# Two fused blocks on one core: who adds the partial sums of the first projection

## The chip, the cores and the metric

The kernel runs as one program on one core of one Trainium2 chip. The metric is the device time of one execution in microseconds (us), taken as the median of several runs. A separately profiled execution gives the trace.

## The reference, cut to what matters

The reference is a network block of two mixer layers (a spatial gating unit, then multi-head latent attention), followed by a second block with its own mixers and a feed-forward part. All of it is float32, for one sequence of 256 positions and a model width of 2048. The change lies in the first projection of the first layer only:

```python
h = rms_norm(x, pre_g[i]) * (1 + scale[:, None, :]) + shift[:, None, :]
u, v, z = jnp.split(h @ w_in, 3, axis=-1)          # w_in: 2048 x 12288
u = jax.nn.gelu(u, approximate=False)
v = layer_norm(jax.nn.gelu(v, approximate=False), norm_g)
```

`shift` and `scale` come from `silu(c) @ ada_w + ada_b`, so `h` is known only as far as the columns of `ada_w` have been summed up.

## The kernel before, in words

**Tiles.** The 256 positions are two tiles `t` of 128 partitions. A float32 product is made of three products: each operand is split into a rounded part `hi` and the rest `lo`, and TensorE adds `hi*hi`, `hi*lo` and `lo*hi` in one bank. The left side of the first projection is held as `a_hi` and `a_lo`. The weights come in slabs of 1 MB (512 rows by 512 columns) into the four places of `raw`; SP issues the loads (`load`, L389), and each waits until the slab four loads before it has been read. A slab of weights is two chunks of 1024 elements per partition. For each chunk `q` ScalarE rounds `hi` (`hi_next`, L565), VectorE subtracts to get `lo` (`lo_next`, L1222), and TensorE runs twelve matmuls (`pe_chunk`, L2237 and L2242), after which `chunk_used` rises. `hi` and `lo` hold four chunks each, so `hi` of chunk `q` waits until chunk `q-4` has been used.

**Phases.** The first 12 column blocks of 512 (eight for `v`, four for the first half of `u`) are computed in four phases, since a quarter of `h` is ready at a time: phase `p` runs all 12 blocks with the rows `4p` to `4p+3` of the 16 row tiles. So there are 48 groups `m = 12p + j`, counted from 0; group `m` is chunks `2m` and `2m+1`. Group `m` writes one of two pairs of banks in turn, and `pe_block` (L2247) waits on `acc_free` until the group before the last one has been read out of its banks. The text calls p = 0 phase 1, and so on to phase 4.

**Read-out.** In phase 1, ScalarE copies the two banks of a group to their place in `v` or `y` (`act_result`, L584). In phases 2 to 4, ScalarE copies the two banks to `stage`, and POOL adds `stage` to the place (`pool_take`, L2088). ScalarE copies group `m` right behind `hi` of chunk `2m+4`, as soon as the group's chunks are used.

**The order of the work** is written out by hand, one queue per engine. In iteration `m` ScalarE does `hi(2m+3)`, `hi(2m+4)`, the read-out of group `m`, and in phase 4 `gelu(j-1)` (L820). VectorE does `lo(2m+3)`, `phase_sum(m+1)`, `lo(2m+4)`, and then small work: in phase 2 copies of turned weights (L1565, L1566), at the end of a phase the next quarter of `h` (L1518 to L1528), in phase 4 the statistics of `v` (L1536). `phase_sum` handles one slab of `ada_w` with four multiply-adds (L1245, L1249), two of them in banks, and every fourth slab with a closing addition (L1254); it is there for j up to 7 of each phase, in phase 4 up to 3. TensorE also has short matmuls between groups (L2316 after j = 3 and 7, transposes L2467 in phase 2). The root and the scaling of the layer norm (L671, L813) stand in ScalarE's queue of phase 4 and POOL multiplies by the gain from then on.

Of the kernel before, what the change touches and what calls it, by code (L numbers as in the profile page):

```python
# [15 lines left out]
ALU = mybir.AluOpType  # L16
# [8 lines left out]
T = 2  # L25
S = 256
D = 2048
KT = D // P
W2 = 4096
NB = 512  # L30
EPS = 1e-6
RAWS = 4
CHUNKS = 4
# [74 lines left out]
PHASES, PHASE_W, PHASE_A, LAST_A = 4, 12, 8, 4  # L108
U_FIRST, U_LAST = 64, 80
FIRST = PHASES * PHASE_W  # L110
MIXED, HEADS_W = 128, 137


PARTIAL = 2 * 3 * PHASE_W
STAGED = PARTIAL + 2 * 59
BEFORE_FFN = STAGED - 8 * 8
LAST_BANKS = 0

# [122 lines left out]
def build(nc, d, out):  # L241
    ctx = ExitStack()
    with ctx:
# [330 lines left out]
        def act_result(act, n, dst, func=ACT.Copy, aset=None, width=NB, normed=False):  # L574

            act.wait_ge(chunk_used, n.chunk.at(CHUNKS))
            if normed:
                act.wait_ge(n_rstd, n.nrm.base)
            for t in range(T):
                s = n.acc.base // 2 % 2 if aset is None else aset  # L580
                if dst is None:
                    act.wait_ge(stage_free, n.stg.at(t + 1))
                to = stage[:, t, :] if dst is None else dst(t)
                nc.scalar.activation(to, ps[:, 2 * s + t, 0:width], func, scale=rstd[:, t:t + 1] if normed else 1.0).then_inc(acc_free, 1)  # L584
            n.acc.base += 2
            if dst is None:
                n.stg.base += 2
# [190 lines left out]
        def _(act):  # L778
# [36 lines left out]
            def gelu(j):  # L815

                for t in range(T):
                    act.wait_ge(stage_free, 2 + PARTIAL - 2 * PHASE_W + 2 * j + t + 1)
                    place = v[:, t, j * NB:(j + 1) * NB] if j < 8 else y[:, t, (j - 8) * NB:(j - 7) * NB]
                    nc.scalar.activation(place, place, ACT.Gelu).then_inc(rounded, 1)  # L820

# [4 lines left out]
            for p in range(PHASES):  # L826
                for j in range(PHASE_W):
                    act_steps(act, n, 2)
                    if p == 0 and j == 2:
                        act.dma_start(ws[:, :, :], d["sgu_w_s"][0].rearrange("g t s -> t g s")).then_inc(ws_landed, 16)  # L830
                    if p < 3 and j == 9:
                        modulated(p + 1)
                        if p == 2:
                            act.dma_start(gain[:, :], d["sgu_norm_g"][0].partition_broadcast(P)).then_inc(gain_landed, 16)
                    if p == 1 and j < 4:
                        place, name = [(rows[:, 0:128], "hg_norm_2"), (rows[:, 128:192], "q_norm_2"), (rows[:, 192:256], "k_norm_2"),
                                       (rows[:, 256:272], "sinks_2")][j]
                        act.dma_start(place, d[name][0].partition_broadcast(P)).then_inc(rows_landed, 16)
                    if p:
                        act_result(act, n, None)  # L840
                    else:
                        act_result(act, n, lambda t: v[:, t, j * NB:(j + 1) * NB] if j < 8 else y[:, t, (j - 8) * NB:(j - 7) * NB])
                    if p == 3 and j:
                        gelu(j - 1)
                        if j == 9:
                            act_root(act, n)
                        if j == 11:
                            scaled(0)
# [365 lines left out]
        def lo_next(dve, n, ahead=AHEAD):  # L1214

            q = n.chunk.base + ahead
            if q >= FFN_CHUNK:
                return lo_planned(dve, q)
            r = raw_of(q)
            dve.wait_ge(hi_ready, n.chunk.at(ahead + 1))  # L1220
            width = chunk_width(q)
            nc.vector.tensor_tensor(lo[:, q % CHUNKS, 0:width], raw[:, r % RAWS, q % 2 * CW:q % 2 * CW + width],  # L1222
                                    hi[:, q % CHUNKS, 0:width].bitcast(F32), ALU.subtract).then_inc(lo_ready, 1)
            if q % 2:
                n.raw.base += 1
# [266 lines left out]
        def _(dve):  # L1492
# [45 lines left out]
            def phase_sum(m):  # L1538

                j = m % PHASE_W  # L1540
                if m < FIRST and j < (PHASE_A if m < FIRST - PHASE_W else LAST_A):
                    ada_sum(dve, n, j % 4, (acc, acc_s)[j // 4], early)

            lo_next(dve, n, 0)
            ada_keep(dve, n, 0, 16)
            modulated(0)
# [4 lines left out]
            for p in range(PHASES):  # L1551
                for j in range(PHASE_W):
                    lo_next(dve, n)
                    n.chunk.base += 1
                    phase_sum(p * PHASE_W + j + 1)
                    lo_next(dve, n)
                    n.chunk.base += 1
                    n.acc.base += 2
                    if j == 5 or p < 3 and j == 8:
                        ada_keep(dve, n, 0, (4 * p + 4 if p < 3 else 32) + (16 if j == 8 else 0))  # L1560
                    if p == 1 and j % 2 and j < 9:
                        q = j // 2
                        dve.wait_ge(sp_turned, q + 1)
                        bank = ps[:, 4, :].rearrange("p (g t) -> p g t", g=4)
                        nc.vector.tensor_copy(wt[:, 4 * q:4 * q + 4, 64:128], bank[:, :, 64:128])  # L1565
                        nc.vector.tensor_copy(wt[0:64, 4 * q:4 * q + 4, 0:64], bank[0:64, :, 0:64]).then_inc(sp_kept, 1)  # L1566
                    if p < 3 and j == 8:
                        modulated(p + 1)
                    if p < 3 and j == 9:
                        split(p + 1)  # L1570
                    if p == 3 and 2 <= j < 10:
                        stats(j - 2)
                    if p == 3 and j == 9:
                        dve.wait_ge(v_ready, 16)
                        for t in range(T):
                            ins = nc.vector.bn_aggr(agg[:, 2 * t:2 * t + 2], cnt[:, t, :, :].rearrange("p a b -> p (a b)"))
                        then(dve, n, ins)
                        nc.vector.tensor_scalar(var[:, :], agg[:, :].rearrange("p (t k) -> p t k", k=2)[:, :, 1], 1.0, EPS, ALU.mult, ALU.add).then_inc(n_var, 1)
                    if p == 3 and j == 10:
                        dve.wait_ge(n_sd, n.nrm.base + 1)  # L1580
                        nc.vector.reciprocal(rstd[:, :], sd[:, :]).then_inc(n_rstd, 1)
                        n.nrm.base += 1
                        dve.wait_ge(n_rstd, n.nrm.base)
                        nc.vector.scalar_tensor_tensor(out=nmr[:, :], in0=agg[:, :].rearrange("p (t k) -> p t k", k=2)[:, :, 0], scalar=-1.0,
                                                       in1=rstd[:, :], op0=ALU.mult, op1=ALU.mult).then_inc(centred, 1)
# [487 lines left out]
        def pool_take(pool, n, op):  # L2073

            for t in range(T):
                pool.wait_ge(acc_free, n.acc.at(5 + t))
                pool.wait_ge(stage_free, n.stg.at(2))
                op(t).then_inc(stage_free, 1)
                n.stg.base += 1
            n.acc.base += 2  # L2080
# [6 lines left out]
        def tt(out_, a, b, op):  # L2087
            return nc.gpsimd.tensor_tensor(out_, a, b, op)  # L2088

        @block.gpsimd  # L2090
        def _(pool):
# [15 lines left out]
            def gained(k):  # L2107

                g = SPATIAL[k]
                for t in range(T):  # L2110
                    pool.wait_ge(ln_scaled, 2 * k + t + 1)
                    piece = v[:, t, g * NB:(g + 1) * NB]
                    tt(piece, piece, gain[:, g * NB:(g + 1) * NB], ALU.mult).then_inc(ln_done, 1)

            n.acc.base = 2 * PHASE_W
            for p in range(1, PHASES):
                for j in range(PHASE_W):
                    place = lambda t: v[:, t, j * NB:(j + 1) * NB] if j < 8 else y[:, t, (j - 8) * NB:(j - 7) * NB]
                    pool_take(pool, n, lambda t: tt(place(t), place(t), stage[:, t, :], ALU.add))
                    if p == 3 and j == 10:  # L2120
                        pool.wait_ge(gain_landed, 16)
                        gained(0)
            gained(1)
            for b in range(4):
                c = slice(b * NB, (b + 1) * NB)
# [297 lines left out]
        def cols(buf, k0=0):  # L2423
            return lambda t, k: buf[:, t, k0 + k * P:k0 + (k + 1) * P]

        @block.tensor
        def _(pe):
# [58 lines left out]
                pe_block(pe, n, A, extra=extra)  # L2486
            pe.wait_ge(vm_act, 8)
            pe.wait_ge(vm_vec, 8)
            pe_blocks_turning(pe, n, A, cols(v), PARTIAL, ada=True, more=True)
            pe_pairs(pe, n, A, 2, ada=True)  # L2490
            pe_blocks_turning(pe, n, B, cols(v, D), PARTIAL + 16, ada=True, stays=True)
            pe.wait_ge(ada_kept, 1 + n.ada.base)
            pe_gate_rows(pe, 0)
            def columns():
# [389 lines left out]
```

## Time and profile before

| what | us |
|---|---|
| median of 3 runs | 2517.88 |
| lowest and highest run | 2517.03, 2519.02 |
| the profiled execution | 2517.61 |
| its span in the trace | 2515.6 |

The span is what the trace covers; 2.0 us of the profiled execution lie around it. Engines are TensorE (PE, with its weight loads PEld), VectorE (DVE), ScalarE (ACT), GpSimd (POOL) and SyncE (SP). A group of instructions is named by its line in the kernel, its engine and its operands. An instruction's duration can reach into the next one's on the same engine, so that starts of neighbours stand closer than their durations.

### The profile page before, as it was taken

The page shows a single profiled execution, that of the slowest core. Times are in us where ns is not written, and L with a number is a line of the kernel's source. Part 1 is how long each engine was busy: PE and PEld are TensorE (multiplying, and loading weights), DVE is VectorE, ACT ScalarE, POOL GpSimd, SP SyncE. Part 2 cuts the span into 40 slices and gives each one's busy share as a digit, 9 for nine tenths or more (in the row PEclk, how much of TensorE's full clock was granted, in tenths as well). Part 3 has the DMA queues.
Part 4 walks back from the last instruction along what each step waited for, and adds up shares of the span by engine and source line. Part 5 has one row for each costly group of instructions (what it writes and reads, how often), then busy time and mean ns, then how long its engine had stood idle before and what let it go on. Part 6 is the DMA issues. An engine that isn't in the chain of part 4 may idle for free.

```text
span 2515.6 us, 31563 instructions
## 1 busy us (share of the span) xinstructions
PE 2465.0 (98%) x11802; PEld 2054.3 (82%) x11802; DVE 1872.2 (74%) x2280; ACT 1403.5 (56%) x1956; POOL 442.1 (18%) x290
## 2 busy tenths in 40 slices
PE   5999999999999999998999999999999999999999
PEld 4888888888887888887888888888888888888887
DVE  7899787866777777766665555557888879888884
ACT  4555764444446655546566667655555645545553
POOL 0065572111021000010000000043111111111111
PEclk9999999999999999999999999999999999999999
DMA  9989777878875877754555554554455564646454
GB/s 349 331 302 337 253 251 270 309 277 283 283 254 181 232 228 215 232 176 142 167 173 162 167 167 150 179 172 170 181 202 200 171 231 167 219 169 222 167 205 157
DMA packets 353477, 547.35 MB, mean 218 GB/s; under 512 B 30684, under 2 KB 124480, under 8 KB 352960
## 3 DMA queue, kind: packets, MB, share of 16 engines
q1 hardware_dynamic: 351520, 539.53, 63.4%
q10 hardware_dynamic: 1824, 6.04, 0.7%
q8 instruction: 84, 1.38, 0.2%
q14 instruction: 49, 0.40, 0.0%
HBM read 543.43 MB, written 2.10 MB: 217 GB/s over the span
## 4 chain that ended last, share of the span: by engine, by line
PE 91%; DVE 5%; ACT 2%; issue 1%; DMA 1%; SPq 0%; DVEq 0%; ACTq 0%; POOL 0%; POOLq 0%
PE ps L2237 50%; PE ps L2242 25%; PE ps L2267 2%; PE ps L2264 2%; PE ps L2263 2%; PE ps L2223 1%; PE ps L2222 1%; PE ps L2224 1%; PE ps L2316 1%; DVE ps L1245 1%; DVE lo L1199 1%; ACT hi L565 1%; DVE lo L1222 1%; PE ps L2840 1%; PE ps L2478 1%
## 5 line engine op out<-in xcount | busy, mean ns | idle before, releaser
L1222 DVE TENSOR_TENSOR lo<-raw,hi 128x1024 fp32r<-128x1024 f32 x550 | 707.7, 1303 | 386.5 <-ACT hi L565 385.7
L565 ACT ACTIVATE hi<-raw 128x1024 fp32r<-128x1024 f32 x550 | 572.3, 1051 | 434.0 <-PE ps L2242 353.2
L2237 PE MATMUL ps<-hi,a_hi 128*128 128x512 f32 (+1 forms) x2016 | 801.0, 397 | 1.2 <-DVE a_lo L1427 0.9
L2237 PE MATMUL ps<-hi,a_lo 128*128 128x512 f32 (+1 forms) x2016 | 785.8, 390 | 0.0
L2242 PE MATMUL ps<-lo,a_hi 128*128 128x512 f32 (+1 forms) x2016 | 539.0, 389 | 0.0
L551 ACT ACTIVATE hi<-raw 128x1024 fp32r<-128x1024 f32 x339 | 358.0, 1060 | 293.1 <-PE ps L2242 254.7
L1199 DVE TENSOR_TENSOR lo<-raw,hi 128x1024 fp32r<-128x1024 f32 x339 | 424.9, 1273 | 107.0 <-ACT hi L551 105.0
L2242 PEld LDWEIGHTS ps<-lo,a_hi 128*128 128x128 f32 x2016 | 378.4, 188 | 79.4
L2237 PEld LDWEIGHTS ps<-hi,a_hi 128*128 128x128 f32 x2016 | 379.0, 188 | 78.8 <-issue 1.9
L2237 PEld LDWEIGHTS ps<-hi,a_lo 128*128 128x128 f32 x2016 | 379.2, 188 | 74.3
L2237 PE MATMUL ps<-hi,b_hi 128*128 128x512 f32 x880 | 348.0, 395 | 0.6 <-ACT y L938 0.3
L2237 PE MATMUL ps<-hi,b_lo 128*128 128x512 f32 x880 | 343.3, 390 | 0.0
L2242 PE MATMUL ps<-lo,b_hi 128*128 128x512 f32 x880 | 235.8, 390 | 0.0
L2088 POOL TENSOR_TENSOR v<-v,stage 128x512 f32<-128x512 f32 (+1 forms) x88 | 149.1, 1695 | 421.8 <-ACT stage L584 281.5
L2242 PEld LDWEIGHTS ps<-lo,b_hi 128*128 128x128 f32 x880 | 165.2, 188 | 35.3
L2237 PEld LDWEIGHTS ps<-hi,b_hi 128*128 128x128 f32 x880 | 165.4, 188 | 34.3 <-issue 0.7
L2237 PEld LDWEIGHTS ps<-hi,b_lo 128*128 128x128 f32 x880 | 165.4, 188 | 33.1
L2088 POOL TENSOR_TENSOR v<-v 128x512 f32<-128x512 f32 x48 | 77.3, 1624 | 593.2 <-ACT v L744 304.7
L1245 DVE SCALAR_TENSOR_TENSOR ps<-raw,cond,ps 128x512 f32<-128x512 f32 x194 | 137.3, 746 | 1.5 <-DMA raw<-in_ada_w 1.5
L2088 POOL TENSOR_TENSOR x<-x,stage 128x512 f32 (+1 forms) x38 | 71.6, 1884 | 332.0 <-DVE stage L1442 310.6
L584 ACT ACTIVATE stage<-ps 128x512 f32<-128x512 f32 x120 | 65.0, 593 | 60.7 <-PE ps L2242 59.7
L2088 POOL TENSOR_TENSOR y<-y,stage 128x512 f32<-128x512 f32 x30 | 52.5, 1751 | 169.2 <-ACT stage L584 167.0
(343 smaller groups left out, 2532.7 us busy)
## 6 DMA issues: line engine op xcount, KB each, us to landing
raw<-in_ada_w SPq DMA_DIRECT2D x96, 1024.0 KB
raw<-in_sgu_w_in SPq DMA_DIRECT2D x96, 1024.0 KB
raw<-in_w_up SPq DMA_DIRECT2D x64, 1024.0 KB
raw<-in_w_down SPq DMA_DIRECT2D x64, 1024.0 KB
raw<-in_w_in SPq DMA_DIRECT2D x42, 1024.0 KB
raw<-in_sgu_w_out SPq DMA_DIRECT2D x32, 1024.0 KB
raw<-in_w_in SPq DMA_DIRECT2D x128, 256.0 KB
raw<-in_mla_w_in SPq DMA_DIRECT2D x32, 512.0 KB
```

Source lines behind the costliest of these rows:

```text
L551: nc.scalar.activation(by_rows(hi[:, q % CHUNKS, :]), raw_piece(place), ACT.Copy).then_inc(hi_ready, 1)
L565: nc.scalar.activation(hi[:, q % CHUNKS, 0:width], raw[:, r % RAWS, q % 2 * CW:q % 2 * CW + width], ACT.Copy).then_inc(hi_ready, 1)
L584: nc.scalar.activation(to, ps[:, 2 * s + t, 0:width], func, scale=rstd[:, t:t + 1] if normed else 1.0).then_inc(acc_free, 1)
L1199: nc.vector.tensor_tensor(by_rows(lo[:, q % CHUNKS, :]), raw_piece(place), by_rows(hi[:, q % CHUNKS, :]).bitcast(F32), ALU.subtract).then_ ...
L1222: nc.vector.tensor_tensor(lo[:, q % CHUNKS, 0:width], raw[:, r % RAWS, q % 2 * CW:q % 2 * CW + width], hi[:, q % CHUNKS, 0:width].bitcast( ...
L1245: ins = nc.vector.scalar_tensor_tensor(out=out[:, :] if a == j == 3 else to, in0=w, scalar=c, in1=to, op0=ALU.mult, op1=ALU.add)
L2088: return nc.gpsimd.tensor_tensor(out_, a, b, op)
L2237: nc.tensor.matmul(ps[:, 2 * s + t, 0:width], x[:, k0 + j, t * P:(t + 1) * P], hi[:, c, w], start=begins, stop=False)
L2242: ins = nc.tensor.matmul(ps[:, 2 * s + t, 0:width], x2[0][:, k0 + j, t * P:(t + 1) * P], lo[:, c, w], start=False, stop=last and j == kts - 1)
L2263: nc.tensor.matmul(ps[:, bank, :], left(j)[0], hi[:, c, w], start=begins and j == 0, stop=False)
L2264: nc.tensor.matmul(ps[:, bank, :], left(j)[1], hi[:, c, w], start=False, stop=False)
L2267: ins = nc.tensor.matmul(ps[:, bank, :], left(j)[0], lo[:, c, w], start=False, stop=ends and j == 1)
```

## The change

ScalarE's copies to `stage` and POOL's additions are gone in phases 2 to 4 of the first projection. VectorE reads each bank and adds it to the place in `v` or `y`. It does group `m-1` in iteration `m`, behind `lo(2m+4)`, and group 47 as well in the last iteration. The addition itself raises `acc_free`; `gelu` on ScalarE waits on `acc_free` in place of `stage_free`. POOL starts at the gain of the layer norm. The counts of `stage_free` are shifted by the additions that are gone (PARTIAL).

```diff
-PARTIAL = 2 * 3 * PHASE_W
-STAGED = PARTIAL + 2 * 59
+STAGED = 2 * 59
...
             def gelu(j):
                 for t in range(T):
-                    act.wait_ge(stage_free, 2 + PARTIAL - 2 * PHASE_W + 2 * j + t + 1)
+                    act.wait_ge(acc_free, 4 + 2 * (FIRST - PHASE_W + j) + t + 1)
...
                     if p:
-                        act_result(act, n, None)
+                        n.acc.base += 2
...
+            def partial_add(m):
+
+                j = m % PHASE_W
+                dve.wait_ge(chunk_used, CHUNKS + 2 * (m + 1))
+                if m == PHASE_W:
+                    dve.wait_ge(acc_free, 4 + 2 * PHASE_W)
+                for t in range(T):
+                    place = v[:, t, j * NB:(j + 1) * NB] if j < 8 else y[:, t, (j - 8) * NB:(j - 7) * NB]
+                    nc.vector.tensor_tensor(place, place, ps[:, m % 2 * 2 + t, :], ALU.add).then_inc(acc_free, 1)
...
                     lo_next(dve, n)
                     n.chunk.base += 1
                     n.acc.base += 2
+                    if p * PHASE_W + j > PHASE_W:
+                        partial_add(p * PHASE_W + j - 1)
+                    if p == PHASES - 1 and j == PHASE_W - 1:
+                        partial_add(p * PHASE_W + j)
...
-            n.acc.base = 2 * PHASE_W
-            for p in range(1, PHASES):
-                for j in range(PHASE_W):
-                    place = lambda t: v[:, t, j * NB:(j + 1) * NB] if j < 8 else y[:, t, (j - 8) * NB:(j - 7) * NB]
-                    pool_take(pool, n, lambda t: tt(place(t), place(t), stage[:, t, :], ALU.add))
-                    if p == 3 and j == 10:
-                        pool.wait_ge(gain_landed, 16)
-                        gained(0)
+            n.acc.base = 2 * FIRST
+            pool.wait_ge(gain_landed, 16)
+            gained(0)
             gained(1)
...
-            pe_blocks_turning(pe, n, A, cols(v), PARTIAL, ada=True, more=True)
+            pe_blocks_turning(pe, n, A, cols(v), 0, ada=True, more=True)
```

## Rows read from the trace of the kernel before

**Rows 1.** Page, part 1: busy us, share of span, instructions by engine.
```profile
PE 2465.0 (98%) x11802; PEld 2054.3 (82%) x11802; DVE 1872.2 (74%) x2280; ACT 1403.5 (56%) x1956; POOL 442.1 (18%) x290
```

**Rows 2.** Window: length; busy PE, PEld, DVE, ACT, POOL; PEclk, DMA share, GB/s.
```profile
117.57:315.05 197.48, 196.99 (x893) 163.18 (x893) 177.43 (x192) 125.15 (x176) 120.42 (x70) 1.00 0.85 298
```

**Rows 3.** Critical chain, TensorE's pieces: start us, length us, what.
```profile
92.65 1.81 PE ps L2237 x8
...
117.57 1.85 PE ps L2237 x8
...
120.34 1.81 PE ps L2237 x8
...
123.06 1.81 PE ps L2237 x8
...
225.33 0.84 PE ps L2316 x8
...
315.05 1.81 PE ps L2237 x8
```

**Rows 4.** Timeline, ScalarE: start us, us, what, idle before and its releaser.
```profile
92.74 1.06 ACT L565 ACTIVATE hi<-raw 128x1024 fp32r<-128x1024 f32 x1 [1.31 <-PE ps L2242]
...
122.52 1.06 ACT L565 ACTIVATE hi<-raw 128x1024 fp32r<-128x1024 f32 x1 [3.31 <-DMA raw<-in_sgu_w_in]
...
262.26 1.28 ACT L820 ACT_TABLE_LOAD   x1
263.56 1.16 ACT L820 ACTIVATE v<-v 128x512 f32<-128x512 f32 x2
```

**Rows 5.** Timeline, VectorE, the same columns.
```profile
93.84 1.23 DVE L1222 TENSOR_TENSOR lo<-raw,hi 128x1024 fp32r<-128x1024 f32 x1 [1.15 <-ACT hi L565]
94.98 0.15 DVE L1261 COPY mod<-ps 128x4 f32<-128x4 f32 x1
...
124.75 0.42 DVE L1565 COPY wt<-ps 128x256 f32<-128x256 f32 x1
...
125.53 1.54 DVE L1222 TENSOR_TENSOR lo<-raw,hi 128x1024 fp32r<-128x1024 f32 x1
...
129.74 0.69 DVE L1254 TENSOR_TENSOR acc<-ps,acc 128x512 f32<-128x512 f32 x1
130.35 1.21 DVE L1222 TENSOR_TENSOR lo<-raw,hi 128x1024 fp32r<-128x1024 f32 x1
...
191.54 2.72 DVE L1245 SCALAR_TENSOR_TENSOR ps<-raw,cond,ps 128x512 f32<-128x512 f32 x4
194.17 3.23 DVE L1222 TENSOR_TENSOR lo<-raw,hi 128x1024 fp32r<-128x1024 f32 x2
```

**Rows 6.** Timeline around one wait of TensorE for VectorE, the same columns.
```profile
809.97 0.42 DVE L1427 TENSOR_TENSOR a_lo<-tf,a_hi 128x256 fp32r<-128x256 f32 x1 [0.72 <-ACT a_hi L733]
...
810.45 0.50 PE L2237 MATMUL ps<-hi,a_hi 128*128 128x512 f32 x1 [0.65 <-DVE a_lo L1427]
...
810.78 0.39 PE L2237 MATMUL ps<-hi,a_lo 128*128 128x512 f32 x1
```

**Rows 7.** Groups of VectorE, 46 to 114 us (phase 1): count, busy us, mean.
```profile
L1222 DVE TENSOR_TENSOR lo<-raw,hi 128x1024 fp32r<-128x1024 f32 x26 | 31.2, 1221 | 9.4 <-ACT hi L565 9.4
L1245 DVE SCALAR_TENSOR_TENSOR ps<-raw,cond,ps 128x512 f32<-128x512 f32 x28 | 19.2, 749 | 1.5 <-DMA raw<-in_ada_w 1.5
```

**Rows 8.** Groups of VectorE and POOL in phase 3 (182 to 248 us).
```profile
L1222 DVE TENSOR_TENSOR lo<-raw,hi 128x1024 fp32r<-128x1024 f32 x24 | 40.3, 1716 | 2.0 <-ACT hi L565 1.8
L1245 DVE SCALAR_TENSOR_TENSOR ps<-raw,cond,ps 128x512 f32<-128x512 f32 x25 | 17.1, 743 | 0.0
...
L2088 POOL TENSOR_TENSOR v<-v,stage 128x512 f32<-128x512 f32 x16 | 23.1, 1446 | 20.3 <-ACT stage L584 19.1
```

**Rows 9.** Windows of 2 us where TensorE idled, columns as in rows 2.
```profile
794.00:796.00 2.00, 0.77 (x3) 0.30 (x2) 2.00 (x4) 1.37 (x6) 0.00 (x0) 1.00 0.25 21
...
1158.00:1160.00 2.00, 0.09 (x1) 0.12 (x1) 2.00 (x7) 1.93 (x8) 0.00 (x0) 0.50 0.00 0
```

More of the change, by code:

```diff
@@ L2488, in _ @@
             pe.wait_ge(vm_vec, 8)
-            pe_blocks_turning(pe, n, A, cols(v), PARTIAL, ada=True, more=True)
+            pe_blocks_turning(pe, n, A, cols(v), 0, ada=True, more=True)
             pe_pairs(pe, n, A, 2, ada=True)
-            pe_blocks_turning(pe, n, B, cols(v, D), PARTIAL + 16, ada=True, stays=True)
+            pe_blocks_turning(pe, n, B, cols(v, D), 16, ada=True, stays=True)
             pe.wait_ge(ada_kept, 1 + n.ada.base)
```

## The prediction, made before the changed kernel was run

> **What bounds the kernel now.** I read the page's first part, then a window over the stretch that the change touches, then the critical chain there, then the timelines of each engine for prices. The page shows TensorE busy for 98% of the span and POOL for 18% [rows 1]: time off ScalarE or POOL is worth nothing unless TensorE waited for it. The window runs from the start of group 13 to the end of phase 4, 197.48 us [rows 2]. TensorE is busy in 196.99 of them at a granted clock of 1.00, its upper level of 2.4 GHz. So there is half a microsecond to win and everything to lose. VectorE is already busy for 177.43 us of the same window. In the critical chain a chunk lasts from 120.34 to 123.06, that is 2.72 us, and a group 5.44 [rows 3]. The 35 groups 13 to 47 make 35 x 5.44 = 190.4 us; the other 7.1 are TensorE's own short work (five column sums of about 0.84 us and three sets of transposes) with its restarts.
>
> **What the change removes.** 72 copies leave ScalarE, which is no bound. 72 additions leave POOL. That helps VectorE: its `lo` subtraction, with both inputs in SBUF, takes 1716 ns in phase 3 while POOL adds, and 1221 ns in phase 1 where POOL is still; the multiply-add that works in a bank takes 743 and 749 [rows 7, 8]. In phase 3 this gives VectorE back 24 x 0.495 = 11.9 us. It is worth nothing by itself, since TensorE did not wait.
>
> **What it adds to VectorE.** Two additions of 128x512, one input in a bank. The nearest row is the closing addition, of the same form: 0.69 us, with the next instruction 0.61 behind its start [rows 5]. A pair is 1.30 us, 72 additions are 72 x 0.61 = 44 us of VectorE's queue, about 15 a phase. The lower bound is this row; above, half of a held-up `lo`, 0.86 us each [rows 8].
>
> **What it moves, the step that decides.** Group m+1 may start only when group m-1 has been read out. ScalarE used to do that while group m ran. Now VectorE does it in iteration m behind `lo(2m+4)`, which needs `hi(2m+4)`, which needs chunk 2m used. From the end of chunk 2m TensorE has only chunk 2m+1 to run, 2.72 us, and then needs the banks. In that time must pass, one after the other:
> - TensorE's end to ScalarE's start: chunk end 92.65, `hi` at 92.74, 0.09 [rows 3, 4];
> - `hi`, 1.06 [rows 4], and its end at 93.80 to `lo` at 93.84, 0.04 [rows 4, 5];
> - `lo` until VectorE takes the next instruction, 93.84 to 94.98, 1.14 [rows 5];
> - the two additions, 0.61 + 0.69 = 1.30 [rows 5];
> - VectorE's end to TensorE: 809.97 + 0.42 = 810.39 to 810.45, 0.06, and the first matmul takes 0.33 to the second instead of 2.72/12 = 0.23, together 0.16 [rows 6].
>
> This is 3.79 us against 2.72: TensorE stops for 1.07 us in every group, though nothing is overloaded. The next chunk follows, so the cycle of a group is 3.79 + 2.72 = 6.51. No lead helps: `hi(2m+4)` has no free place earlier. It holds for groups 14 to 48, which wait for the additions of groups 12 to 46: 35 cycles, 227.9 us.
>
> VectorE's own queue in a group with a slab of `ada_w`: from the end of chunk 2m+1 at 2.72, `hi(2m+5)` and signals, `lo(2m+5)` starts at 2.72 + 0.09 + 1.06 + 0.04 = 3.91, and the additions let go at 1.19 + 1.14 + 1.22 = 3.55, before it. Then 1.14 and four multiply-adds, 191.54 to 194.17, 2.63 [rows 5]: `lo(2m+6)` can start at 7.68, and the cycle wants it at 6.51 + 1.19 = 7.70. Both limits meet, so whatever is added to this queue now costs. Added are:
> - the closing addition (j = 2 and 6 in phases 2 and 3, j = 2 in phase 4): 5 x 0.61 = 3.1 us;
> - the copies in phase 2, 124.75 to 125.53, 0.78 [rows 5], start at 3.55 and push `lo(2m+5)` from 3.91 to 4.33: three times with a slab behind them, 3 x 0.42 = 1.3 us;
> - the first read-out: `hi(30)` came 122.52 - 120.34 = 2.18 us after chunk 26, held by its DMA, not 0.09 [rows 3, 4]: 2.1 us once. Later slabs have a longer cycle to land in, so I charge the DMA queue of SP nothing more; without that cover it is the DMA's pace of before, 5.44 a group, below the new cycle;
> - phase 4, j = 1 to 2: `gelu` now waits for VectorE's addition and ScalarE's `hi(2m+5)` stands behind it. The first addition ends at 1.19 + 1.14 + 0.69 = 3.02; a table load of 1.28 and two gelus of 1.16 [rows 4] end at 5.46, and `lo(2m+5)` starts at 6.56, not at 3.91. If the load is made ahead of the wait it is some 1.1 less. Behind it is the last slab sum: 1.5 to 2.6, I take 2.1. Without such a sum, in the other groups of phase 4, `hi(2m+5)` is done by 5.4 and `hi(2m+6)` only starts at 6.6, which hides gelus and statistics;
> - the root at j = 9 with its two tables: nothing to 2 x 1.28 = 2.6, I take 1.2, near one load [rows 4].
>
> These make 9.8 us. POOL's gain multiplications start earlier if at all, and the last two additions stand where VectorE used to wait for `hi(99)`: nothing, as long as the lead of three chunks is there; without it they cost their 1.3 us.
>
> **The sum.** The window becomes 227.9 + 9.8 = 237.7 us. TensorE's short work falls into the stops, so it is not added. Less 197.48 this is 40.2 us more. The profiled execution took 2517.61 (span 2515.6 and 2.0 around it); 2517.6 + 40.2 = 2557.8, and the median of the runs is only 0.3 above that execution. Nothing later gives it back, TensorE being full. I say 2558.
>
> **The rivals.** *Not slower.* The queues alone are counted: a group with a slab costs VectorE 2 x 1.14 + 2.63 + 1.30 = 6.21 against 5.44, eight groups a phase, 8 x 0.77 = 6.2 us behind, and a lead of three chunks, 8.2 us, swallows that before the light groups make it up. Then the banks come free in time and the run stays at 2518. It decides itself at 2.72 us from the end of chunk 2m to the second addition's end. For it: VectorE gets 11.9 us back. Against: the pieces of that path sum to 3.63 even without the restart, and the lead does not apply to it. 5%: 3 for no change, 2 for a small gain out of the time given back.
>
> *Half the stop.* Signals and restart cost nothing and part of `lo` is ready when the bank wait is looked at: 35 x 0.5 + 5 = 23 us, 2541. Against it stands each row above. 8%.
>
> *ScalarE gets stuck in phase 4.* If every gelu and every round of `hi` changes the table, 2 x 1.28 a group, less the 1.2 us that ScalarE has spare, cost 11 x 1.36 = 15 us more, 2573; with the additions at 0.86 each (35 x 0.5 = 17) it is 2590. The row shows a table load once there, not a load per group. 14%.
>
> *The clock falls.* TensorE now stops once a group. Where it idled longer the trace shows both: with 0.77 us busy in 2, the granted clock is 1.00; in 1158 to 1160, after several microseconds with little work, it is 0.50, the lower level of 1.2 GHz [rows 9]. Stops of 1.07 in 6.51 are far milder than the first, so I expect 2.4 GHz. If it fell every second cycle, two chunks of 5.44 would take the place of 6.51: 17 x 4.4 = 75 us more, 2633. 6%. The Trainium skill, page "TensorE: Matmul & The Clock Gate", section "A second HAM failure mode: psum-queue depth-cycling", says that short idles of TensorE between groups that take turns in the banks can make the clock go back and forth; by that rule this change would bring this case, and no row here shows it at such short stops.
>
> **Chances.** The forecast has 67%. Its own range: all signals and extras at their least give about 2542 (35 x 0.3 and 5 less), the additions at their upper bound 2575. Taking in half the stop and the first part of the stuck ScalarE, the range is 2538 to 2580. A measurement of this kernel tells some 0.2% (5 us) from no change. Faster 0.02, same 0.03, slower 0.95.
>
> **What would show it.** In the profile after: TensorE waiting for VectorE's additions into `v` and `y` some 35 times, about 1 us each; in the chain the pattern TensorE, `hi`, `lo`, two additions, TensorE; groups 6.5 us apart also for j above 7, where VectorE is not loaded, which tells the forecast from any count of queues; the additions near 690 ns, 72 of them; `lo` back at 1.22; clock 1.00. It is wrong if TensorE's waits are missing, if they stand only at j below 8, or if its matmuls are slow.

## The result and the profile after

The changed kernel takes 2563.55 us (median of 4 runs, 2562.33 to 2564.83) against 2518.07 for the kernel before in the same measurement: 1.0178 times as long, 95% interval 1.0166 to 1.0190, so 45.5 us or 1.8% slower. The forecast was 2558 (40 us slower), in a range of 2538 to 2580. Of all the executions reported below one, of add_first, took 3551.37 us at a mean granted clock of 0.656, and it is left out of the intervals.

| | before | after |
|---|---|---|
| span in the trace, us | 2515.6 | 2560.5 |
| start of the first spatial matmul, us | 320.33 | 365.38 |

Up to group 13 the two traces run alike. The first spatial matmul, TensorE's first one of the stage behind this projection, stands two chunks behind the end of phase 4. It comes 45.05 us later, and the span is 44.9 us longer. So the whole loss lies in the cycles from group 13 on, before groups 14 to 48 start, and nothing is given back or added later. I use this start as the yardstick below, since it leaves out what other stages of a single run do.

The page's first part, to be read against [rows 1]:

```profile
PE 2475.4 (97%) x11802; PEld 2053.4 (80%) x11802; DVE 1886.5 (74%) x2352; ACT 1371.9 (54%) x1884; POOL 313.8 (12%) x218
```

ScalarE has lost 32 us of work, POOL 128; VectorE has only 14 more, though 72 additions came to it. TensorE has the same 11802 matmuls, and yet 10.4 us more of busy time, in a span that is 44.9 longer. Where these 10 us come from is told with the size of the cycle below.

The window from the start of group 13 to that of group 48, as in [rows 2]:

```profile
core 0: us, PE busy (x) PEld busy (x) DVE busy (x) ACT busy (x) POOL busy (x), PEclk, DMA share, GB/s
117.33:359.84 242.51, 207.77 (x896) 162.85 (x894) 195.46 (x264) 95.74 (x108) 0.00 (x0) 0.99 0.71 246
```

It is 242.51 us long where it was 197.48, with TensorE busy for 207.77: a stretch that had half a microsecond of idle time now has 35, and its busy time is 10.8 longer with it. VectorE, the engine that took the work, is busy 195 of 243, less densely than before.

TensorE's waits in that stretch (what waited, for whom, us in total, times, the longest):

```profile
PE ps L2245 <- DVE v L1551: 23.9, 24, 2.8
PE ps L2245 <- DVE y L1551: 8.9, 9, 1.1
```

33 waits for the additions into `v` and `y`, 32.8 us. Two more stops of 0.99 us, at 194.46 and 275.82, have no releaser in the trace and stand at the same place in their groups; that makes one before each of the groups 14 to 48, 35 in all. The critical chain over one group, j = 8 of phase 3, where no slab of `ada_w` loads VectorE; it answers to [rows 3]:

```profile
249.05 2.11 PE ps L2245 x8
251.16 0.92 PE ps L2250 x4
252.08 0.02 issue
252.10 0.02 ACTq L562
252.11 0.04 issue
252.16 1.07 ACT hi L564
253.23 0.02 issue
253.25 1.23 DVE lo L1221
254.48 1.20 DVE v L1551 x2
255.68 0.04 issue
255.73 2.11 PE ps L2245 x8
```

Here is the path as forecast: chunk, `hi`, `lo`, two additions, chunk. From 249.05 to 255.73 is 6.68 us, where it was 5.44. Of the 34 distances between the pairs of additions of the groups 12 to 46, 27 lie between 6.67 and 6.77 us. The others are two that the next sections explain (8.55 and 8.27 in phase 4), four of 7.20 to 7.54 that mostly hold a closing addition more, and one of 6.81.

VectorE's groups over phase 3 of this kernel, which answer to [rows 8]:

```profile
L1221 DVE TENSOR_TENSOR lo<-raw,hi 128x1024 fp32r<-128x1024 f32 x24 | 29.4, 1223 | 13.7 <-ACT hi L564 13.3
L1244 DVE SCALAR_TENSOR_TENSOR ps<-raw,cond,ps 128x512 f32<-128x512 f32 x26 | 17.8, 749 | 0.0
L1551 DVE TENSOR_TENSOR v<-v,ps 128x512 f32<-128x512 f32 x16 | 10.2, 680 | 0.0
```

`lo` is back at 1223 ns from 1716, with the multiply-add in a bank unchanged. This agrees with the Trainium skill, page "SBUF — State Buffer", section "Who interferes with whom": by it a VectorE instruction with two inputs in SBUF competes with a GpSimd instruction that reads SBUF, and one with at most one such input, outside its 2-port modes, does not. An addition takes 680 ns, two of them follow at 0.60.

### The profile page after: what moved, and what is told of

Read it like the earlier page. It is cut to its first block, busy times and chain, and to the rows that moved or that the text cites. A ratio compares the mean times of both kernels' runs of the same rounds, so it can differ in the third digit from the quotient of the medians.

```text
span 2560.5 us, 31384 instructions
## 1 busy us (share of the span) xinstructions
PE 2475.4 (97%) x11802; PEld 2053.4 (80%) x11802; DVE 1886.5 (74%) x2352; ACT 1371.9 (54%) x1884; POOL 313.8 (12%) x218
## 4 chain that ended last, share of the span: by engine, by line
PE 85%; DVE 9%; ACT 3%; issue 2%; DMA 1%; SPq 0%; ACTq 0%; DVEq 0%; POOL 0%; POOLq 0%
PE ps L2245 46%; PE ps L2250 23%; DVE lo L1221 2%; PE ps L2275 2%; PE ps L2272 2%; PE ps L2271 2%; ACT hi L564 2%; DVE ps L1244 1%; DVE v L1551 1%; DMA raw<-in_sgu_w_in 1%; PE ps L2231 1%; PE ps L2230 1%; PE ps L2232 1%; DVE lo L1198 1%; PE ps L2324 1%
## 5 line engine op out<-in xcount | busy, mean ns | idle before, releaser
L1221 DVE TENSOR_TENSOR lo<-raw,hi 128x1024 fp32r<-128x1024 f32 x550 | 681.7, 1252 | 418.8 <-ACT hi L564 417.7
L1198 DVE TENSOR_TENSOR lo<-raw,hi 128x1024 fp32r<-128x1024 f32 x339 | 424.5, 1272 | 107.0 <-ACT hi L550 104.9
L2101 POOL TENSOR_TENSOR v<-v,stage 128x512 f32<-128x512 f32 (+1 forms) x40 | 66.9, 1672 | 257.1 <-ACT stage L583 234.4
L1244 DVE SCALAR_TENSOR_TENSOR acc_b<-raw,cond,acc_b 128x512 f32<-128x512 f32 x90 | 73.5, 816 | 0.0
L2101 POOL TENSOR_TENSOR v<-v,gain 128x512 f32<-128x512 f32 x16 | 22.5, 1428 | 386.4 <-ACT v L812 386.4
```

The costliest lines, as they stand in the source:

```text
L1198: nc.vector.tensor_tensor(by_rows(lo[:, q % CHUNKS, :]), raw_piece(place), by_rows(hi[:, q % CHUNKS, :]).bitcast(F32), ALU.subtract).then_ ...
L1244: ins = nc.vector.scalar_tensor_tensor(out=out[:, :] if a == j == 3 else to, in0=w, scalar=c, in1=to, op0=ALU.mult, op1=ALU.add)
```

## The experiments

All kernels are the changed one with an edit, except two that edit the kernel before. The times of before and after are medians of four executions, the others of a single one unless an interval stands beside them. The kernel before gave 2520.93 us in the measurement of the first four, 2518.35 in that of the next two, 2518.49 in that of the last four.

| kernel | us | first spatial matmul, us | TensorE waited on the read-outs |
|---|---|---|---|
| before | 2518.07 | 320.33 | none |
| after | 2563.55 | 365.38 | 33 times, 32.8 us |
| short_sums | 2558.62 | 361.48 | 33 times, 28.4 us |
| short_adds | 2539.71 | 342.77 | 13 times, 10.8 us |
| late_copy | 2530.25 | 332.89 | 5 times, 7.2 us |
| add_mid | 2534.57 | 336.52 | 14 times, 9.9 us |
| add_early | 2526.66 | 330.07 | 12 times, 5.7 us |
| add_first | 2521.20 | 324.04 | 6 times, 3.0 us |
| after_again | 2561.62 | 364.54 | 33 times, 32.0 us |
| gelu_later | 2559.47 | 362.39 | 33 times, 31.5 us |
| late_copy2 | 2526.28 | 327.14 | 4 times, 2.8 us |
| first_short | 2517.71 | 319.51 | none |

### Is it the path or VectorE's load?

**short_sums** takes load off VectorE and leaves the path alone.

```diff
-                w, c = raw[:, k, j * NB:(j + 1) * NB], cond[:, 4 * a + j:4 * a + j + 1]
+                w, c = raw[:, k, j * NB:j * NB + (64 if narrow else NB)], cond[:, 4 * a + j:4 * a + j + 1]
...
-                    ada_sum(dve, n, j % 4, (acc, acc_s)[j // 4], early)
+                    ada_sum(dve, n, j % 4, (acc, acc_s)[j // 4], early, m > PHASE_W)
```

> The changed kernel with the multiply-adds of phase_sum for groups 13 and up cut from 512 to 64 columns (the columns of shift, scale and gate that come from them are left out, so those values are not the reference's). Theory of the path (chunk end, hi, lo, two additions, TensorE): VectorE's queue in a group shrinks by some 2 us, and yet every group still stops, since the path does not hold the sums. Cycles stay at 6.7 us; only the surplus in groups with a closing addition (some 3 us in all) and part of the long stop at j = 2 of phase 4 go: 2556 to 2561. Rival, VectorE's queue is full: 20 groups give back 1 us and more each, 2535 to 2543.

It took 2558.62, and the spatial matmuls start 3.9 us earlier than after the change alone. The starts of the additions of neighbouring groups still lie about 6.7 us apart. The exception is the first distance, 8.29 us, with a stop of 3.09 us, behind which the granted clock fell to 0.50. Taking 2 us of work out of VectorE's queue in each of 19 groups gave back no more than the surplus of a few of them: in the other groups VectorE only waited longer for `hi`. The rival of a full queue is out as the cause of the 6.7.

**short_adds** shortens the path.

```diff
-                    nc.vector.tensor_tensor(place, place, ps[:, m % 2 * 2 + t, :], ALU.add).then_inc(acc_free, 1)
+                    nc.vector.tensor_tensor(place[:, 0:64], place[:, 0:64], ps[:, m % 2 * 2 + t, 0:64], ALU.add).then_inc(acc_free, 1)
```

> The changed kernel with each addition over 64 of its 512 columns (the rest of v and u keeps only phase 1's part). Path theory: each pair gets 2 x 448 / 0.96 GHz shorter, by the measured 0.60 from start to start some 0.45 to 0.47 us an addition, 0.9 a group, and the cycle falls by the same, 6.7 to 5.8; 35 groups, -32 us: 2528 to 2534. Rival, the stop comes from the wait and not from its length: no change in the light groups, 2550 or more.

It took 2539.71, some 6 above the expectation's upper end, 3 of which are that chip's kernel before. The light groups did what was expected: 5.74 to 5.80 us, from 6.69. The groups with a slab did not all follow: most lie at 5.7 to 6.8, the first at 7.51, and two of phase 4 at 8.02 and 7.34, with a stop of 2.29 us and a granted clock of 0.50 behind it. The critical chain of a group with a slab runs through VectorE's queue:

```profile
214.91 2.72 DVE ps L1244 x4
217.64 1.13 DVE lo L1221
218.76 0.27 DVE v L1551 x2
```

So with the path shortened the queue holds these groups, the second limit that the prediction had just beside the first. The critical chain over a light group, the same columns as above:

```profile
175.49 0.01 issue
175.50 2.14 PE ps L2245 x8
177.63 0.92 PE ps L2250 x4
178.55 1.81 PE ps L2245 x8
180.37 0.91 PE ps L2250 x4
181.27 0.01 issue
181.28 2.14 PE ps L2245 x8
```

TensorE now stands still for 0.01 us, and the group from 175.50 to 181.28 still takes 5.78 and not 5.44. The path is shorter, but it is still there: the first chunk ends at 178.55, and `hi`, `lo` and the short additions take the 2.73 us to 181.28. This is the term that my sum had too small; the section on the prediction returns to it.

**Where in the queue.** Three kernels move the additions forward in VectorE's iteration; only the last pair, of group 47, stays. The load is the same in all of them. The edits in short, with `m` for the iteration's group and the condition left out:

```diff
 add_mid:                       add_early:                     add_first:
                                                              +    partial_add(m - 1)
     lo_next(dve, n)                lo_next(dve, n)                lo_next(dve, n)
                               +    partial_add(m - 1)
     phase_sum(m + 1)               phase_sum(m + 1)               phase_sum(m + 1)
+    partial_add(m - 1)
     lo_next(dve, n)                lo_next(dve, n)                lo_next(dve, n)
-    partial_add(m - 1)        -    partial_add(m - 1)        -    partial_add(m - 1)
```

> The changed kernel with partial_add(m-1) between phase_sum(m+1) and lo(2m+4). Path theory: without a slab the additions end 3.6 us after chunk 2m-1, with 5.44 to spare: no stops at j above 7 and in most of phase 4. With a slab, 3.6 + 2.6 + 0.3 = 6.5 against 5.44: 20 groups stop by about 1 us and the closing additions add 3: 2535 to 2545. Rival, one place in the queue is as good as another: 2563.

> The changed kernel with partial_add(m-1) right behind lo(2m+3), ahead of phase_sum. Path theory: the additions end some 3.6 us after chunk 2m-1 and the banks are wanted at 5.44, so the stops in the light groups vanish; what is left is VectorE's load in the groups with a slab (6.2 us against 5.44), of which 1.8 us a phase is swallowed by the lead: 2523 to 2535. Rival, VectorE's additional 44 us of work are what costs: near 2563.

> The changed kernel with partial_add(m-1) at the head of iteration m, ahead of lo(2m+3). The additions then run while ScalarE rounds hi(2m+3), and the banks are free about 1.4 us after chunk 2m-1, 4 us before they are wanted. VectorE's load in the groups with a slab stays: phases 2 and 3 fall 5 to 8 us behind, less the 4 that are to spare. Path theory: 2518 to 2526, at or a little above the kernel of before. Rival, the load of VectorE is what costs: 2545 and more.

add_mid came at 2534.57, just under its range; add_early at 2526.66 (6 runs; 1.0033 times the kernel before, 1.0021 to 1.0045); add_first at 2521.20 (11 runs; 1.0009, 1.0000 to 1.0018). In add_mid and add_early the light groups of phase 4 run at 5.44 us again; in add_first TensorE does not wait in them either. One place further forward each time, and 28.9 of the 45.05 us, then 35.3, then 41.3 are gone, by the yardstick, with not one instruction less for VectorE. It is the place of the additions that costs, not the additions. All TensorE's waits in add_first:

```profile
PE ps L2245 <- DVE v L1551: 3.0, 6, 0.9
```

**first_short** asks for the rest of add_first, 3.7 us by the yardstick. It is add_first with short_sums' narrow multiply-adds.

> add_first and short_sums together: additions at the head of the iteration, and the multiply-adds of phase_sum for groups 13 and up on 64 of 512 columns (those parts of shift, scale and gate are left out). Path theory: neither the path nor VectorE's load holds TensorE, so the window is as in the kernel of before, 2515 to 2520, and 1 to 5 us under add_first. Rival, each addition costs TensorE something wherever it stands (its banks, its port): 2521 and more.

It took 2517.71 (10 runs; 0.9997 times the kernel before, 0.9987 to 1.0007), the spatial matmuls start at 319.51, and TensorE never waits in the stretch. So what add_first had left was VectorE's load in the groups with a slab, and an addition that meets neither limit costs nothing.

### Does a late read-out cost by itself?

**late_copy** leaves the work of before where it was, ScalarE and POOL, and puts ScalarE's read-out off by one group in phases 2 and 3. The lines left out of the cut read the last group of phase 3 out in time.

```diff
-                    if p:
+                    if p in (1, 2):
+                        if p * PHASE_W + j > PHASE_W:
+                            n.acc.base -= 2
+                            n.chunk.base -= 2
+                            act_result(act, n, None)
+                            n.chunk.base += 2
+                        n.acc.base += 2
...
+                    elif p:
                         act_result(act, n, None)
```

> The kernel of before, with ScalarE reading out group m-1 behind hi(2m+4) in phases 2 and 3, one iteration later than it did, POOL adding as before. Path theory: chunk end 0.09, hi 1.06, two copies 1.09, 0.06 to TensorE is 2.3 us, below the 2.72 of a chunk: no stop in groups with j above 7. In groups with a slab of ada_w hi(2m+4) was 2.2 us late for its DMA in the kernel of before, so there some stops come: +4 to +14 us, 2522 to 2532. Rival, any read-out that is put off by a group stops TensorE in each of the 22 groups: +24 us or more.

The time, 2530.25, is in the range, but in part for a wrong reason. Three of its five stops in the timeline (start us, us, what, idle before and its releaser):

```profile
123.97 0.50 PE L2247 MATMUL ps<-hi,a_hi 128*128 128x512 f32 x1 [1.09 <-ACT stage L584]
...
130.84 0.50 PE L2247 MATMUL ps<-hi,a_hi 128*128 128x512 f32 x1 [0.70 <-ACT stage L584]
...
174.98 0.50 PE L2247 MATMUL ps<-hi,a_hi 128*128 128x512 f32 x1 [2.46 <-ACT stage L584]
```

I had put the copies behind the activations for the next quarter of `h` at j = 9, some 3 us of ScalarE's work, and there the path is long: a stop of 2.46 us at 174.98 and another at 248.19, and the granted clock is below 1.00 behind both (0.52 and 0.55 in the lowest windows of 2 us). **late_copy2** puts them ahead of those activations.

```diff
+                    if p in (1, 2) and p * PHASE_W + j > PHASE_W:
+                        n.acc.base -= 2
+                        n.chunk.base -= 2
+                        act_result(act, n, None)
+                        n.chunk.base += 2
                     if p < 3 and j == 9:
                         modulated(p + 1)
...
-                    if p:
+                    if p in (1, 2):
+                        n.acc.base += 2
...
```

> The kernel of before with ScalarE's read-out put off by a group as in late_copy, but ahead of the four activations for the next quarter of h at j = 9. Path theory: the two stops of 2.5 us behind those activations go, and with them the fallen clock; light groups run at 5.44 without a stop, though their read-out is a group late. The distance to the spatial matmuls is 4 to 7 us above the kernel of before instead of 12.6: 2522 to 2527. Rival, a late read-out costs by itself: 2530 as late_copy.

It took 2526.28, 6.8 us above before by the yardstick, 1.9 of which are one wait at the spatial matmuls for POOL. The long stops are gone. Three of the four that are left, all in groups with a slab:

```profile
123.78 0.50 PE L2247 MATMUL ps<-hi,a_hi 128*128 128x512 f32 x1 [1.03 <-ACT stage L584]
...
130.65 0.50 PE L2247 MATMUL ps<-hi,a_hi 128*128 128x512 f32 x1 [0.69 <-ACT stage L584]
...
144.09 0.50 PE L2247 MATMUL ps<-hi,a_hi 128*128 128x512 f32 x1 [0.88 <-ACT stage L584]
```

The fourth is one of 0.25 us at the end of phase 3's slabs. The light groups run without a stop for the read-out, though the banks are read out a group late as in the changed kernel. In one of them, in phase 3, `hi` starts at 239.12 and the two copies end at 241.15, some 2.1 us after the end of the chunk and 0.4 before the next group is due. The changed kernel's path of 3.65 us does not fit: it is the length of the path against one chunk that decides.

### Phase 4

**gelu_later** moves `gelu(0)` to the next iteration, beside `gelu(1)`.

```diff
-                    if p == 3 and j:
+                    if p == 3 and j > 1:
+                        if j == 2:
+                            gelu(0)
                         gelu(j - 1)
```

> The changed kernel with gelu(0) of phase 4 done one iteration later, beside gelu(1). Path theory: hi(2m+5) no longer waits for gelu(0) ahead of the last slab sum, so the 8.55 us cycle becomes 7.2 (the closing addition stays), and without the stop of 2.8 us the clock has no cause to fall, 1.6 us more: 3 us less than the changed kernel, its trace's distance from group 13 to the spatial matmuls 245 us instead of 248. Rival, phase 4 is slow for its statistics: no change.

The timeline of the changed kernel at this place shows the mechanism:

```profile
286.68 1.28 ACT L819 ACT_TABLE_LOAD   x1
...
287.84 1.28 DVE L1551 TENSOR_TENSOR v<-v,ps 128x512 f32<-128x512 f32 x2
288.55 1.23 ACT L819 ACTIVATE v<-v 128x512 f32<-128x512 f32 x2 [0.59 <-DVE v L1551]
...
289.17 0.50 PE L2245 MATMUL ps<-hi,a_hi 128*128 128x512 f32 x1 [0.95 <-DVE v L1551]
...
289.68 1.04 ACT L564 ACTIVATE hi<-raw 128x1024 fp32r<-128x1024 f32 x1
...
290.76 1.23 DVE L1221 TENSOR_TENSOR lo<-raw,hi 128x1024 fp32r<-128x1024 f32 x1 [1.65 <-ACT hi L564]
...
295.26 1.22 DVE L1221 TENSOR_TENSOR lo<-raw,hi 128x1024 fp32r<-128x1024 f32 x1
296.39 1.28 DVE L1551 TENSOR_TENSOR v<-v,ps 128x512 f32<-128x512 f32 x2
...
297.73 0.57 PE L2245 MATMUL ps<-hi,a_hi 128*128 128x512 f32 x1 [2.82 <-DVE v L1551]
```

The table is loaded ahead of the wait. ScalarE's gelus wait for the addition of 287.84; `hi` starts only at 289.68 behind them, `lo` at 290.76, the last slab sum and the second `lo` follow, and TensorE has stopped for 2.82 us at 297.73. In gelu_later that cycle is 7.21 and not 8.55, the next 6.67 and not 8.27 (that one is the clock, see below), and the spatial matmuls start 3.0 us earlier, as expected; the time is 2559.47. Only 1.34 of the 3.0 are shown to be the edit's: 1.6 are the fallen clock, and in after_again, without this edit, that cycle took 6.70 as well.

**after_again** is the changed kernel a second time.

> The changed kernel, unedited, as a second look beside the three others of this job. The stops are the same 35 with the same 6.7 us cycle. If the fallen clock behind the long stop in phase 4 hangs on chance, it may be missing or stand behind the first stop of 2.7 us instead: 2561 to 2567.

It took 2561.62. The windows of 2 us behind its two longest stops stand beside those of the first trace of the same kernel. The columns are the length of the window, then busy time and count of PE, PEld, DVE, ACT and POOL, then the granted clock, DMA share and GB/s. The first trace:

```profile
296.00:298.00 2.00, 0.27 (x1) 0.27 (x2) 2.00 (x4) 0.89 (x2) 0.00 (x0) 1.00 1.03 385
298.00:300.00 2.00, 2.00 (x6) 1.56 (x6) 1.55 (x3) 1.29 (x2) 0.00 (x0) 0.50 0.51 199
300.00:302.00 2.00, 2.00 (x8) 1.57 (x7) 0.54 (x1) 0.00 (x0) 0.00 (x0) 0.64 0.21 30
124.00:126.00 2.00, 0.25 (x1) 0.25 (x2) 2.00 (x5) 0.19 (x1) 0.00 (x0) 1.00 0.98 366
126.00:128.00 2.00, 2.00 (x10) 1.59 (x10) 2.00 (x4) 0.00 (x0) 0.00 (x0) 1.00 0.86 312
```

The second trace:

```profile
124.00:126.00 2.00, 0.30 (x1) 0.30 (x2) 2.00 (x5) 0.14 (x1) 0.00 (x0) 1.00 1.02 384
126.00:128.00 2.00, 2.00 (x6) 1.51 (x5) 2.00 (x3) 0.00 (x0) 0.00 (x0) 0.56 0.78 285
128.00:130.00 2.00, 2.00 (x7) 1.59 (x6) 2.00 (x4) 0.00 (x0) 0.00 (x0) 0.58 0.95 339
296.00:298.00 2.00, 0.00 (x0) 0.00 (x0) 2.00 (x4) 0.14 (x1) 0.00 (x0) 1.00 1.03 381
298.00:300.00 2.00, 1.52 (x7) 1.26 (x8) 1.62 (x3) 2.00 (x3) 0.00 (x0) 1.00 0.90 348
```

Both traces have a stop of 2.7 to 2.8 us that ends near 125.7 (2.73 and 2.80) and one of 2.82 that ends near 298. In the first trace the clock falls to 0.50 (1.2 GHz) behind the second and stays at 1.00 behind the first; in the second trace it is the other way round. What it costs is one longer cycle each time, 8.27 against 6.70 and 8.27 against 7.48. In gelu_later there is a stop of 2.85 at 125.72, and the clock stays at 1.00.

## Why the prediction was right, and where a size was off

**What bounds the kernel, and what is removed:** right. TensorE had nothing to lose but its fullness; the relief of VectorE came (1716 to 1223 ns) and gained nothing.

**The path:** right, and shown from both sides: shortened by 0.9 us it gives 0.9 us a group back (short_adds, light groups), moved forward it vanishes with all its work still done (add_first, first_short), and a late read-out with a short path costs nothing (late_copy2).

**The size of the cycle:** 6.51 forecast, 6.69 measured, 35 x 0.18 = 6.3 us, the main error. The step that was mis-sized is the last piece, "and the first matmul takes 0.33 to the second instead of 2.72/12 = 0.23, together 0.16" with "The next chunk follows, so the cycle of a group is 3.79 + 2.72 = 6.51". The 2.72 is the pitch at which chunks follow one another. The path needs the time from a chunk's first matmul to the end of its last, and the chain of after shows it: the chunk that starts at 249.05 ends at 252.08, 3.03 us later. In a full stream a matmul lasts 0.39 but follows the other at 0.23, so the pitch leaves out 0.16 of the last one's tail; the first matmuls behind a wait add 0.15, where I had 0.10. The rest of the path, 252.08 to 255.73, took 3.65, where I had 3.69. These 0.31 us a group are time in which TensorE counts as busy: in 35 groups they make 10.9 us, near the 10.4 by which its busy time grew. In short_adds, where the idle time has shrunk to 0.01 us, they are still there: 3.05 for the chunk and 2.73 for the path make 5.78 against 5.44.

**The extras:** 9.8 forecast, some 6.5 measured. Group 13 takes 8.42 us from its start at 117.33 to the 125.75 at which group 14 starts, so the first read-out cost 1.7 and not 2.1. The closing additions cost about 0.5 each, not 0.61; the copies of phase 2 about 0.7 in all, not 1.3. At j = 2 of phase 4 the surplus is 8.55 - 6.69 = 1.9 with its closing addition, where I had 2.7: the table load ran ahead of the wait, the lower of my two bounds. The root at j = 9 cost 0.1 and not 1.2: its table load fell into idle time of ScalarE, and the load for the next gelu, at 350.33, ran ahead of its wait. On top comes the fall of the clock, 1.6, which the sum did not have. Together: 6.3 more from the cycle, 3.3 less from the extras, 1.6 more from the clock, is 4.6; measured are 45.05 less the forecast's 40.2, 4.85.

**The rivals.** *Not slower* is out by the 35 stops, *half the stop* by their length, 0.94 us and more in most. *ScalarE gets stuck in phase 4* happened in one group instead of eleven, and gelu_later shows it. *The clock falls* happened behind one stop, not at every second group; that it happened at all was not in the sum. The section of the Trainium skill named in the prediction, "A second HAM failure mode: psum-queue depth-cycling" of "TensorE: Matmul & The Clock Gate", would have had the short stops between groups bring it on; in this trace it does not agree: 27 stops of 0.94 to 1.47 us, each followed by 5.7 us of matmuls or more, went by without a fall of the granted clock from 1.00.

**The signs named beforehand** came as told, with 35 stops and TensorE's short work inside the cycles as forecast (behind the five column sums the stop is only 0.16 us long), but for the additions, at 680 ns instead of 690, and the clock, not 1.00 throughout. The light groups 6.7 us apart were the one that mattered.

## What to carry to other kernels

When a read-out of an accumulator moves to another engine's queue, do not count only the load: write down what stands ahead of it there and on what that waits, and compare the path from the event that starts it to the moment the banks are wanted. If the read-out stands behind work for the chunks ahead, it inherits that work's wait; put it at the head of the iteration, where here the same additions cost 4 us and not 45. And in such a path take a chunk's time from its first matmul to the end of its last, not its pitch in a full stream.

## What the runs showed of the hardware that was not expected

The idle time that the trace shows before a matmul understates what a late wait costs. It counts from the end of the last matmul, 0.16 us behind the point at which the next one starts in a full stream, and the first matmuls behind the wait are slower. With 0.01 us of idle time a group of 24 matmuls took 5.78 us instead of 5.44 (short_adds). A wait that is met before that point costs nothing that the trace shows: the light groups of late_copy2 ran at a full stream's pace.

The length of a stop alone did not tell whether TensorE's clock would fall behind it. Of the same two stops of 2.7 to 2.8 us in the same kernel, one was followed by 0.50 in one trace and the other in the next, at about 0.8 to 1.6 us each; it was chance as far as these runs show. Behind the 27 stops of 0.94 to 1.47 us of the changed kernel, with 5.7 us of matmuls between them, it did not fall. But a stop of 1.69 us in add_mid passed at 1.00, and one of 1.49 us in add_early, right behind the column sum (L2324, eight matmuls of one column), did not. The matmul in add_early's timeline that ended the stop, and a window behind it with the columns named under after_again:

```profile
279.07 0.50 PE L2245 MATMUL ps<-hi,a_hi 128*128 128x512 f32 x1 [1.49 <-DVE v L1551]
...
280.00:282.00 2.00, 2.00 (x6) 1.55 (x5) 2.00 (x4) 0.62 (x1) 0.00 (x0) 0.50 1.03 397
```
